# Scores of a recurrence step in two blocks of 64 queries in place of four blocks of 32

## The chip, the cores and the metric

The kernel runs on one core of one Trainium2 chip. The metric is the device time of one execution in microseconds, the median of several runs. TensorE (PE) multiplies 128x128 blocks of weights with streams of columns, and its weight loads are profiled apart as PEld. VectorE (DVE), ScalarE (ACT) and GpSimd (POOL) do the elementwise work, and SyncE (SP) issues transfers. The engines run their own programs and wait for each other on semaphores.

## What is computed

One step of a two-layer decoder trunk for 1024 prompt tokens and 64 sample tokens (8 sequences of 8). The first layer is a pooling mixer, the second gated linear attention with four heads of key width 128 and value width 512. All is float32. What the change touches is the recurrence of a head over the prompt. The reference does it in chunks of 32 tokens:

```python
bcum = jnp.cumsum(lg, axis=3)                 # log decay within a chunk
q_dec = q * jnp.exp(bcum)
k_intra = k * jnp.exp(-bcum)
k_state = k * jnp.exp(blast - bcum)
att = jnp.where(causal, jnp.einsum('nbhid,nbhjd->nbhij', q_dec, k_intra), 0.0)
o_intra = jnp.einsum('nbhij,nbhje->nbhie', att, v)
def step(s, inp):
    qc, kc, vc, dc = inp
    o_inter = jnp.einsum('bhid,bhde->bhie', qc, s)
    s = dc[..., None] * s + jnp.einsum('bhjd,bhje->bhde', kc, vc)
    return s, o_inter
```

The result does not hang on the length of the chunk: a score of query i and key j is the sum over d of q[i] k[j] exp(L[i] - L[j]), L being the running sum of the log decay. Any token's L can be taken off both sides, as long as neither exponential gets too large.

## The kernel before

Each engine has its program written out by hand, and the order in it is fixed. In the second layer a head goes through: projections of queries and keys, log decay, value rows for all tokens, then the recurrence over eight steps of 128 tokens (`SUP`), then gates, norm and output projection. The work of the heads on PE is written out four times; on the other engines the later heads are loops.

In the recurrence PE runs, for each step: a part of the gate projections as filling (`fill`), the scores of the next step (`scores(s + 1)`), a transposition of the next step's decayed keys (`key_rows`), the output of this step (`output`: scores times values, then queries times state), the state's update (`update`), another filling, and later the small products for the sample tokens. Products of the projections are split in a high and a low part of type f32r, three products each, all at L549.

The scores of a step are made in blocks of `CH` = 32 queries, so four in a step of 128. Block b has a copy of the keys of its own, `Kp[:, b, :]`, in which the decay of the keys is measured from the last token ahead of the block. Keys behind the block are zeros, set once a head by a memset of all of Kp at L960. To make a step's blocks

- ACT (`exps`, L1171) writes exp(-(L[j] - L[reference])) into the first 32 (b + 1) columns of block b, for four blocks with 32, 64, 96 and 128 columns; the first block needs no reference. It waits for PE's scores of the step before (`att_done`), since there is one Kp;
- POOL (`scale_kp`, L966) multiplies the blocks with the keys kT, four instructions of the same widths, once the last exponential is done;
- DVE (`qd_args`, L1459 and L1460) writes L[i] - L[reference] for the queries into qd, a copy for the first block and a subtraction for the other three; ACT takes the exponential (L1175), and DVE multiplies with the queries (`scale_qk`, L1468);
- PE (`scores`, L1842) multiplies each block of Kp (weights, 128x128) with its 32 columns of qd into a part of the PSUM bank X[0], four matmuls in f32, when Kp and qd are there and the scores of the step before are read;
- DVE (`att_out`, L1481) copies the causal half of the 128x128 scores to `att`.

Other work of a step on these engines: ACT evacuates gates (L1213), transposed keys (L1190) and outputs (L1202, L1203) and takes the exponential for `qs` (L1184), the queries that meet the state; DVE scales qs (L1474) and updates the state; POOL sums squares (L975, L977) and makes the low parts of weights (L344). At a head's end Kp also holds the rows of the sample tokens, all 512 columns, which are multiplied at L1924 with 64 columns of an identity. `att_hi` and `att_lo` at L1919 are the sample tokens' scores in two parts, 64 columns each. L417 is the sum of squares between the layers, matmuls with a single column.

Of the kernel before, what the change touches and what calls it, by code (L numbers as in the profile page):

```python
# [24 lines left out]
P = 128  # L25
# [13 lines left out]
WE = BUF + TP + NB * SEG  # L39
SE0 = BUF + TP  # L40
RANK = 16
CH = 32
SUP = 4 * CH
NSUP = TP // SUP
EPS = 1e-6
NC_ = 1 + NB
# [45 lines left out]
def trunk(nc, x_prompt, x_sample, c_prompt, c_sample, state_pool, state_gla, ada_w, ada_b, norm_g,  # L92
# [8 lines left out]
    with ctx:  # L101
        def sb(name, shape, dt=f32, stack=ctx):
            return stack.enter_context(nc.sbuf_tensor(name, shape, dt))
# [50 lines left out]
        S = sb("S", [P, GW])  # L154
        qd = sb("qd", [P, SUP])
        qs = sb("qs", [P, SUP])
        ks = sb("ks", [P, SUP])
        ksT = sb("ksT", [P, 2, P])
        att = sb("att", [P, 2, SUP])
        att_s = sb("att_s", [P, NS])  # L160
# [25 lines left out]
        L = sb("L", [P, T], stack=heads)  # L186
        Kp = sb("Kp", [P, 4, SUP], stack=heads)
        ki_s = sb("ki_s", [P, NS], stack=heads)
# [52 lines left out]
        def sem(name):  # L241
            return ctx.enter_context(nc.semaphore(name))
# [44 lines left out]
        kp_zero, kp_exp, kp_ready = sem("kp_zero"), sem("kp_exp"), sem("kp_ready")  # L287
# [17 lines left out]
        def units(plan, g, n):  # L305

            return g * plan.units + n + 3
# [9 lines left out]
        def wait_apart(eng, what, count):  # L317


            count = eng.to_reg(count)  # L320
            eng.wait_ge(vec_ready, 1)
            eng.wait_ge(what, count)
# [18 lines left out]
        def lo_slots(lay, plan, eng, g, j):  # L341

            eng.wait_ge(lay.hi_done, g * plan.slots + j + 1)
            nc.gpsimd.tensor_tensor(slot_lo(plan, j), stage[:, j % 2, :], slot_hi(plan, j).bitcast(f32),  # L344
                                    ALU.subtract).then_inc(lay.lo_done, 1)
# [531 lines left out]
        def _(pool):  # L877
# [71 lines left out]
            def head(g, first):  # L949
                if first:  # L950
                    pool.wait_ge(h_ready, 8)
                    pool.wait_ge(hs_low_ready, 8)
                for j in range(2 if first else 0, GP.slot["Z0"] + 1):
                    if j == GP.slot["V0"]:
                        pool.wait_ge(L1.evac[0], g * GP.in_set[0] + GP.place[GP.unit["Q"]] + 1)
                        pool.wait_ge(L1.evac[1], g * GP.in_set[1] + GP.place[GP.unit["K"]] + 1)
                    lo_slots(L1, GP, pool, g, j)

                wait_apart(pool, L1.unit_done, units(GP, g, GP.unit["LG"] + 1))
                pool.memset(Kp[:], 0.0).then_inc(kp_zero, 1)  # L960

                def scale_kp(s):

                    pool.wait_ge(kp_exp, g * NSUP + s + 1)
                    for b in range(4):
                        last = pool.tensor_tensor(Kp[:, b, 0:CH * (b + 1)], Kp[:, b, 0:CH * (b + 1)],  # L966
                                                  kT[:, s * SUP:s * SUP + CH * (b + 1)], ALU.mult)
                    last.then_inc(kp_ready, 1)

                def square_sum(s):  # L970

                    n = P if s < NSUP else NS
                    q = sqo[s % 2]
                    pool.wait_ge(osq_ready, g * (NSUP + 1) + s + 1)
                    pool.tensor_tensor(q[:, 0:2 * n], q[:, 0:2 * n], q[:, 2 * n:4 * n], ALU.add).then_inc(chain_p, 1)  # L975
                    pool.wait_ge(chain_p, s + 1)
                    pool.tensor_tensor(q[:, 0:n], q[:, 0:n], q[:, n:2 * n], ALU.add).then_inc(osum_ready, 1)  # L977

                scale_kp(0)
                lo_slots(L1, GP, pool, g, GP.slot["Z1"])  # L980
                scale_kp(1)
                for s in range(NSUP + 1):
                    if s + 2 < NSUP:
                        scale_kp(s + 2)
                    if s == 1:
                        lo_slots(L1, GP, pool, g, GP.slot["Z2"])
                    if s == 5:
                        lo_slots(L1, GP, pool, g, GP.slot["Z3"])
                    square_sum(s)
                pool.wait_ge(ksm_ready, (g + 1) * NB)  # L990
                lo_slots(L1, GP, pool, g, GP.slot["O01"])
                for j in range(GP.slot["O23"], GP.slots):
                    lo_slots(L1, GP, pool, g, j)
                pool.sem_clear(chain_p)

            head(0, True)
            with pool.Fori(1, NG) as g:
                head(g, False)
# [3 lines left out]
        def _(act):  # L1002
# [117 lines left out]
            def head(g, first):  # L1120
# [21 lines left out]
                for t, (n0, w) in enumerate(NT):  # L1142
                    last = nc.scalar.activation(L[:, n0:n0 + w], ps[GP.set[u]][:, t, 0:w], ACT.Identity,
                                                bias=vecT[:, ds(g + V_BG, 1)])
# [20 lines left out]
                def exps(s):  # L1165
                    c0 = s * SUP
                    if s >= 1:
                        act.wait_ge(att_done, g * NSUP + s)
                    for b in range(4):
                        kw = {} if b == 0 else {"bias": L[:, c0 + CH * b - 1:c0 + CH * b]}  # L1170
                        last = nc.scalar.activation(Kp[:, b, 0:CH * (b + 1)], L[:, c0:c0 + CH * (b + 1)], ACT.Exp,  # L1171
                                                    scale=-1.0, **kw)
                    last.then_inc(kp_exp, 1)
                    act.wait_ge(qd_arg, g * NSUP + s + 1)
                    nc.scalar.activation(qd[:], qd[:], ACT.Exp).then_inc(qd_exp, 1)  # L1175
                    if s >= 1:
                        act.wait_ge(kT_done, g * NSUP + s)
                    nc.scalar.activation(ks[:], L[:, c0:c0 + SUP], ACT.Exp, scale=-1.0,
                                         bias=L[:, c0 + SUP - 1:c0 + SUP]).then_inc(ks_exp, 1)
# [36 lines left out]
                def high(i):  # L1216

                    act.wait_ge(gated, g * KG + i + 1)
                    nc.scalar.activation(a_hi[:, i, :], oT[:, i, :], ACT.Copy).then_inc(gated_hi, 1)

                exps(0)
                exp_qs(0)
                split_slot(L1, GP, act, g, GP.slot["Z1"])
                act.wait_ge(smp_kT, g + 1)
                nc.scalar.activation(ksT_s[:], ps[1][:, 1, 0:P], ACT.Copy).then_inc(smp_ksT, 1)
                ksT_out(0)
                exps(1)
                for s in range(NSUP):
                    if s in (0, 4):
                        gate_in(s // 4)  # L1230
                    if s + 1 < NSUP:
                        ksT_out(s + 1)
                    if s + 2 < NSUP:
                        exps(s + 2)
                    o_out(s)
                    if s + 1 < NSUP:
                        exp_qs(s + 1)
                    if s in (1, 5):
                        split_slot(L1, GP, act, g, GP.slot["Z2"] + s // 4)
# [8 lines left out]
                                     scale=1.0 / GW)  # L1248
                nc.scalar.activation(rms_cols[0:NS, NSUP:NSUP + 1], X[0][0:NS, P + NSUP:P + NSUP + 1], ACT.Sqrt,
                                     bias=eps[0:NS, 0:1], scale=1.0 / GW).then_inc(orms_ready, 1)  # L1250
# [20 lines left out]
            for s in range(NSUP + 1):  # L1271
                n = P if s < NSUP else NS
                act.wait_ge(yT_done, s + 1)
                if s:
# [5 lines left out]
                                     scale=1.0 / D).then_inc(y_root, 1)  # L1280
# [3 lines left out]
        def _(dve):  # L1284
# [140 lines left out]
            with dve.Fori(0, NG) as g:  # L1425
# [28 lines left out]
                def qd_args(s):  # L1454

                    c0 = s * SUP
                    if s >= 1:
                        dve.wait_ge(att_done, g * NSUP + s)
                    nc.vector.tensor_copy(qd[:, 0:CH], L[:, c0:c0 + CH])  # L1459
                    nc.vector.tensor_tensor(qd[:, CH:SUP].rearrange("p (b t) -> p b t", b=3),  # L1460
                                            L[:, c0 + CH:c0 + SUP].rearrange("p (b t) -> p b t", b=3),
                                            L[:, c0 + CH - 1:c0 + SUP - 1:CH].unsqueeze(2).broadcast_to([P, 3, CH]),
                                            ALU.subtract).then_inc(qd_arg, 1)

                def scale_qk(s):
# [85 lines left out]
                att_out(0)  # L1551
                dve.wait_ge(smp_ksT, g + 1)
                qd_args(1)
                scale_qk(1)
                for s in range(NSUP + 2):
# [56 lines left out]
        def _(pe):  # L1612
# [178 lines left out]
            def head(g, first):  # L1791
# [42 lines left out]
                def scores(s):  # L1834
                    pe.wait_ge(kp_ready, g * NSUP + s + 1)
                    pe.wait_ge(qd_ready, g * NSUP + s + 1)
                    if s >= 1:
                        pe.wait_ge(att_ready, g * NSUP + s)
                    else:
                        pe.wait_ge(smp_attr, g + 1)  # L1840
                    for b in range(4):
                        last = nc.tensor.matmul(X[0][:, b * CH:(b + 1) * CH], Kp[:, b, :], qd[:, b * CH:(b + 1) * CH],  # L1842
                                                start=True, stop=True)
                    last.then_inc(att_done, 1)
# [185 lines left out]
```

## Time and profile before

| | us |
|---|---|
| median of 3 runs | 1652.73 |
| lowest and highest of the runs | 1651.33, 1653.35 |
| span of the profiled execution, first to last instruction | 1651.1 |
| PE busy in it | 1613.4 |

What lies around the span is not in the profile; the runs shown are 0.2 to 2.3 us longer than it. The layers follow each other: the pooling layer to about 750 us, norm and first projections to about 850 us, then the four heads of about 213 us each, with a recurrence of some 70 us in each, and the last norm from about 1625 us.

Matmuls are pipelined: a record lasts from the start of its matmul to the drain of its last column, so records overlap, and what one costs the engine is read from its start to the start of the next. An f32 matmul shows as two records. A wait in the trace is put down to the one that ended it last.

### The profile page before, as it was taken

Reading aid. Unit: us, or ns where it says so; the run is one execution under the profiler, and the core shown is the slowest. Engines: PE = TensorE matmul, PEld = TensorE weight load, DVE = VectorE, ACT = ScalarE, POOL = GpSimd, SP = SyncE. Lnnn points to the kernel's source line nnn. Section 1 sums busy time; section 2 is a strip of 40 time slices with the busy share of each in tenths; the row PEclk is TensorE's granted clock in tenths of the full one; section 3 lists DMA queues with packets and bytes.
Section 4 is the critical chain, followed back from the end, with each engine's and each line's share of the span. In section 5 each row is a group of like instructions: output and inputs, shape, how many; then the busy total and the mean of one; then the engine's idle time right before and its main releaser. Section 6 shows DMA issues by size and latency. Waiting matters only on the chain.

```text
span 1651.1 us, 25118 instructions
## 1 busy us (share of the span) xinstructions
PE 1613.4 (98%) x9827; PEld 1501.1 (91%) x9827; DVE 818.7 (50%) x1271; ACT 458.2 (28%) x969; POOL 375.8 (23%) x384
## 2 busy tenths in 40 slices
PE   6999999999999999998999999999999999999996
PEld 5899999999999999998788898888998989979896
DVE  4654449443944475457224562245622356224475
ACT  4321112111211121123325413154040541315423
POOL 3022212211211212211314223133130322314310
PEclk8999999999999999998999999999999999999998
DMA  9512221221122121210202212022120221201312
GB/s 330 193 56 87 62 63 42 84 74 42 55 78 64 57 67 54 77 41 27 64 18 73 84 40 77 13 64 84 53 66 12 64 96 40 77 13 40 110 37 108
DMA packets 137545, 115.03 MB, mean 70 GB/s; under 512 B 6013, under 2 KB 120281, under 8 KB 137442
## 3 DMA queue, kind: packets, MB, share of 16 engines
q1 hardware_dynamic: 135616, 112.87, 22.0%
q8 instruction: 78, 1.28, 0.3%
q10 hardware_dynamic: 1834, 0.74, 0.2%
q14 instruction: 17, 0.14, 0.0%
HBM read 99.05 MB, written 15.00 MB: 69 GB/s over the span
## 4 chain that ended last, share of the span: by engine, by line
PE 94%; DVE 3%; SPq 1%; DMA 1%; ACT 1%; issue 0%; ACTq 0%; DVEq 0%
PE psA L549 40%; PE psB L549 29%; PE psB L1804 8%; PE psA L1804 4%; PE psB L1860 2%; PE psB L1877 2%; PE psX L1842 2%; PE psB L1868 2%; PE psX L1897 1%; DVE a_hi L637 1%; PE psB L1909 1%; PE psX L1720 1%; DMA ada<-in_ada_w 1%; DVE y_rows L1606 0%; PE psB L1910 0%; PE psX L1661 0%
## 5 line engine op out<-in xcount | busy, mean ns | idle before, releaser
L344 POOL TENSOR_TENSOR w_lo<-stage,w_hi 128x1024 fp32r<-128x1024 f32 x100 | 249.7, 2496 | 891.1 <-ACT w_hi L339 891.1
L339 ACT ACTIVATE w_hi<-stage 128x1024 fp32r<-128x1024 f32 x100 | 107.0, 1070 | 433.7 <-PE psB L549 297.6
L549 PE MATMUL psA<-h_hi,w_hi 128*128 128x362 f32 (+1 forms) x864 | 210.9, 349 | 4.1 <-DVE h_lo L453 3.8
L549 PE MATMUL psA<-h_lo,w_hi 128*128 128x362 f32 (+1 forms) x864 | 193.6, 329 | 0.0
L549 PE MATMUL psA<-h_hi,w_lo 128*128 128x362 f32 (+1 forms) x864 | 193.1, 329 | 0.0
L549 PEld LDWEIGHTS psA<-h_hi,w_hi 128*128 128x128 f32 x864 | 151.4, 190 | 27.1 <-issue 21.2
L549 PEld LDWEIGHTS psA<-h_hi,w_lo 128*128 128x128 f32 x864 | 151.5, 190 | 0.0
L549 PEld LDWEIGHTS psA<-h_lo,w_hi 128*128 128x128 f32 x864 | 151.4, 190 | 0.0
L549 PE MATMUL psA<-a_hi,w_hi 128*128 128x362 f32 (+1 forms) x480 | 109.7, 334 | 2.6 <-DVE a_lo L640 1.9
L549 PE MATMUL psB<-h_hi,w_hi 128*128 128x362 f32 (+1 forms) x480 | 109.7, 331 | 0.0
L549 PE MATMUL psB<-h_hi,w_lo 128*128 128x362 f32 (+1 forms) x480 | 107.9, 327 | 0.0
L549 PE MATMUL psB<-h_lo,w_hi 128*128 128x362 f32 (+1 forms) x480 | 107.7, 327 | 0.0
L549 PE MATMUL psA<-a_hi,w_lo 128*128 128x362 f32 (+1 forms) x480 | 106.4, 327 | 0.0
L549 PE MATMUL psA<-a_lo,w_hi 128*128 128x362 f32 (+1 forms) x480 | 106.4, 327 | 0.0
L549 PE MATMUL psB<-a_hi,w_hi 128*128 128x362 f32 (+1 forms) x480 | 106.0, 329 | 0.0
L549 PE MATMUL psB<-a_hi,w_lo 128*128 128x362 f32 (+1 forms) x480 | 105.2, 327 | 0.0
L549 PE MATMUL psB<-a_lo,w_hi 128*128 128x362 f32 (+1 forms) x480 | 105.1, 327 | 0.0
L966 POOL TENSOR_TENSOR Kp<-Kp,kT 128x32 f32<-128x32 f32 (+3 forms) x128 | 45.5, 385 | 219.2 <-ACT Kp L1171 219.2
L549 PEld LDWEIGHTS psA<-a_hi,w_hi 128*128 128x128 f32 x480 | 82.7, 188 | 7.3 <-DVE a_lo L640 4.7
L549 PEld LDWEIGHTS psB<-h_hi,w_hi 128*128 128x128 f32 x480 | 82.9, 189 | 2.5 <-issue 2.4
L549 PEld LDWEIGHTS psB<-h_hi,w_lo 128*128 128x128 f32 x480 | 83.7, 188 | 0.0
L549 PEld LDWEIGHTS psB<-h_lo,w_hi 128*128 128x128 f32 x480 | 83.5, 188 | 0.0
(345 smaller groups left out, 2790.6 us busy)
## 6 DMA issues: line engine op xcount, KB each, us to landing
stage<-in_gla_w_in SPq DMA_DIRECT2D x40, 512.0 KB, 3.8
stage<-in_pool_w_in SPq DMA_DIRECT2D x32, 512.0 KB, 4.1
ada_stage<-in_ada_w SPq DMA_DIRECT2D x24, 512.0 KB, 3.8
ada<-in_ada_w SPq DMA_DIRECT2D x16, 512.0 KB, 8.4
stage<-in_pool_w_out SPq DMA_DIRECT2D x16, 512.0 KB, 3.4
v<-in_state_gla SPq DMA_DIRECT2D x32, 256.0 KB, 2.6
out_new_gla_sample<-v SPq DMA_DIRECT2D x32, 256.0 KB, 2.1
stage<-in_gla_w_out SPq DMA_DIRECT2D x16, 512.0 KB, 3.7
```

Of the source, the lines that this page charges most:

```text
L339: nc.scalar.activation(slot_hi(plan, j), stage[:, j % 2, :], ACT.Copy).then_inc(lay.hi_done, 1)
L344: nc.gpsimd.tensor_tensor(slot_lo(plan, j), stage[:, j % 2, :], slot_hi(plan, j).bitcast(f32), ALU.subtract).then_inc(lay.lo_done, 1)
L549: last = nc.tensor.matmul(ps[u][:, t, 0:width], weight(w[:, p, :], k), a[:, k, n0:n0 + width], start=(k == 0 and pas == 0), stop=(k == kt ...
L637: nc.vector.tensor_copy(a_hi[:, i, c], oT[:, i, c]).then_inc(chain_v, 1)
L966: last = pool.tensor_tensor(Kp[:, b, 0:CH * (b + 1)], Kp[:, b, 0:CH * (b + 1)], kT[:, s * SUP:s * SUP + CH * (b + 1)], ALU.mult)
L1720: last = nc.tensor.matmul(X[1][rows, P:2 * P], csT[:, k * NC_:k * NC_ + CG], ada_stage[:, k, :], start=(k < 4), stop=(k >= 4))
L1804: last = nc.tensor.matmul(ps[GP.set[u]][0:n, j, :], h[:, k, s * P:s * P + n], w[k // 2][:, c], start=(k == 0 and pas == 0), stop=(k == KD ...
L1842: last = nc.tensor.matmul(X[0][:, b * CH:(b + 1) * CH], Kp[:, b, :], qd[:, b * CH:(b + 1) * CH], start=True, stop=True)
L1860: last = nc.tensor.matmul(ps[1][:, 0, e * P:(e + 1) * P], v[:, s, e * P:(e + 1) * P], att[:, s % 2, :], start=(e == 0), stop=(s == 0 and e ...
L1868: last = nc.tensor.matmul(ps[1][:, 0, e * P:(e + 1) * P], S[:, e * P:(e + 1) * P], qs[:], start=False, stop=(e == KG - 1), skip_group_chec ...
L1877: nc.tensor.matmul(ps[1][:, 2, :], ksT[:, s % 2, :], v[:, s, :], start=True, stop=True).then_inc(upd_done, 1)
L1897: last = nc.tensor.matmul(X[1][rows, :], qd_cols[:, c:c + CG], v[:, b, :], start=first, stop=not first)
```

## The change

A block has 64 queries in place of 32, so a step of 128 tokens has two blocks. The decay of both keys and queries of a block is measured from the middle token of the block (`MID` = 31), in place of the token ahead of it, so that no exponent spans more than 32 tokens, as before. Blocks 2 and 3 of Kp are no longer written in a step; the tile keeps its size, since the sample tokens' rows need it. The memset covers only what is never written: columns 64 to 127 of block 0.

```diff
-CH = 32
-SUP = 4 * CH
+CH = 64
+MID = CH // 2 - 1
+SUP = 2 * CH
...
-                pool.memset(Kp[:], 0.0).then_inc(kp_zero, 1)
+                pool.memset(Kp[:, 0, CH:SUP], 0.0).then_inc(kp_zero, 1)
...
-                    for b in range(4):
+                    for b in range(2):
                         last = pool.tensor_tensor(Kp[:, b, 0:CH * (b + 1)], Kp[:, b, 0:CH * (b + 1)],
                                                   kT[:, s * SUP:s * SUP + CH * (b + 1)], ALU.mult)
...
-                    for b in range(4):
-                        kw = {} if b == 0 else {"bias": L[:, c0 + CH * b - 1:c0 + CH * b]}
+                    for b in range(2):
+                        mid = c0 + CH * b + MID
                         last = nc.scalar.activation(Kp[:, b, 0:CH * (b + 1)], L[:, c0:c0 + CH * (b + 1)], ACT.Exp,
-                                                    scale=-1.0, **kw)
+                                                    scale=-1.0, bias=L[:, mid:mid + 1])
...
-                    nc.vector.tensor_copy(qd[:, 0:CH], L[:, c0:c0 + CH])
-                    nc.vector.tensor_tensor(qd[:, CH:SUP].rearrange("p (b t) -> p b t", b=3),
-                                            L[:, c0 + CH:c0 + SUP].rearrange("p (b t) -> p b t", b=3),
-                                            L[:, c0 + CH - 1:c0 + SUP - 1:CH].unsqueeze(2).broadcast_to([P, 3, CH]),
+                    nc.vector.tensor_tensor(qd[:].rearrange("p (b t) -> p b t", b=2),
+                                            L[:, c0:c0 + SUP].rearrange("p (b t) -> p b t", b=2),
+                                            L[:, c0 + MID:c0 + SUP:CH].unsqueeze(2).broadcast_to([P, 2, CH]),
                                             ALU.subtract).then_inc(qd_arg, 1)
...
-                    for b in range(4):
+                    for b in range(2):
                         last = nc.tensor.matmul(X[0][:, b * CH:(b + 1) * CH], Kp[:, b, :], qd[:, b * CH:(b + 1) * CH],
                                                 start=True, stop=True)
```

PE's program around the scores of a step in the middle of a recurrence, before; psX is the bank of the scores, the line after them transposes the decayed keys:

```order
L549 MATMUL psA<-h_hi,w_lo 128x362 x2
L1842 MATMUL psX<-qd,Kp 128x32 x4
L1852 MATMUL psB<-ident,ks 128x128
L1860 MATMUL psB<-att,v 128x128 x4
L1868 MATMUL psB<-qs,S 128x128 x4
L1877 MATMUL psB<-v,ksT 128x512
```

The same place now:

```order
L550 MATMUL psA<-h_hi,w_lo 128x362 x2
L1842 MATMUL psX<-qd,Kp 128x64 x2
L1852 MATMUL psB<-ident,ks 128x128
L1860 MATMUL psB<-att,v 128x128 x4
L1868 MATMUL psB<-qs,S 128x128 x4
L1877 MATMUL psB<-v,ksT 128x512
```

Four matmuls of 32 columns have become two of 64; nothing before or behind them has moved.

POOL's program where it makes the blocks of steps 0 and 1, before:

```order
L960 MEMSET Kp 128x512
L966 TENSOR_TENSOR Kp<-Kp,kT 128x32
L966 TENSOR_TENSOR Kp<-Kp,kT 128x64
L966 TENSOR_TENSOR Kp<-Kp,kT 128x96
L966 TENSOR_TENSOR Kp<-Kp,kT 128x128
L344 TENSOR_TENSOR w_lo<-stage,w_hi 128x1024
```

and now:

```order
L961 MEMSET Kp 128x64
L967 TENSOR_TENSOR Kp<-Kp,kT 128x64
L967 TENSOR_TENSOR Kp<-Kp,kT 128x128
L345 TENSOR_TENSOR w_lo<-stage,w_hi 128x1024
L967 TENSOR_TENSOR Kp<-Kp,kT 128x64
```

The blocks of 32 and 96 columns are gone on POOL, and likewise on ACT; the order of the rest stays.

## Rows read from the trace of the kernel before

**Rows 1.** The page, busy time of each engine (share of the span), instructions:

```profile
PE 1613.4 (98%) x9827; PEld 1501.1 (91%) x9827; DVE 818.7 (50%) x1271; ACT 458.2 (28%) x969; POOL 375.8 (23%) x384
```

**Rows 2.** Windows of the recurrences: stretch, length, busy by engine, PEclk, DMA share, GB/s:

```profile
850.00:925.00 75.00, 75.00 (x492) 66.67 (x491) 31.69 (x86) 36.43 (x95) 26.73 (x48) 1.00 0.24 78
...
1489.00:1564.00 75.00, 75.00 (x492) 66.67 (x491) 31.49 (x86) 36.54 (x95) 26.69 (x49) 1.00 0.24 78
```

**Rows 3.** Waits of PE from 800 to 1640 us: total us, times, longest:

```profile
PE psB L1804 <- ACT kT L1127: 1.4, 3, 0.5
```

**Rows 4.** Groups of PE by shape, 850 to 1640 us: busy us, mean ns, idle before:

```profile
L1842 PE MATMUL psX<-qd,Kp 128*128 128x32 f32 x256 | 31.1, 265 | 0.0
```

**Rows 5.** Timeline of PE in the last head's recurrence: start us, length us, instruction:

```profile
1500.79 0.97 PE L1842 MATMUL psX<-qd,Kp 128*128 128x32 f32 x8
...
1506.47 0.97 PE L1842 MATMUL psX<-qd,Kp 128*128 128x32 f32 x8
1507.28 0.31 PE L1852 MATMUL psB<-ident,ks 128*128 128x128 f32 x1
...
1508.31 1.06 PE L1868 MATMUL psB<-qs,S 128*128 128x128 f32 x8
...
1513.27 0.97 PE L1842 MATMUL psX<-qd,Kp 128*128 128x32 f32 x8
```

**Rows 6.** Timeline of PE at the third recurrence's end, matmuls of 64 columns:

```profile
1348.01 0.19 PE L1919 MATMUL psX<-att_hi,v_s 128*128 128x64 f32 x1
1348.04 0.27 PE L1919 MATMUL psX<-att_lo,v_s 128*128 128x64 f32 x1
...
1348.82 1.08 PE L1924 MATMUL psX<-ident,Kp 128*128 128x64 f32 x8
1349.71 0.47 PE L1909 MATMUL psB<-v_s,ksm 128*128 128x512 f32 x1
```

**Rows 7.** Groups by shape in the last head, 1430 to 1640 us, as in rows 4:

```profile
L1171 ACT ACTIVATE Kp<-L 128x128 f32<-128x128 f32 x8 | 3.1, 388 | 0.0
L1171 ACT ACTIVATE Kp<-L 128x64 f32<-128x64 f32 x8 | 2.7, 336 | 0.0
L1468 DVE TENSOR_TENSOR qd<-qd,qT 128x128 f32<-128x128 f32 x8 | 2.3, 290 | 9.6 <-ACT qd L1175 9.6
L1460 DVE TENSOR_TENSOR qd<-L 128x96 f32<-128x96 f32 x8 | 2.0, 251 | 0.0
L1459 DVE COPY qd<-L 128x32 f32<-128x32 f32 x8 | 1.5, 182 | 0.0
...
L966 POOL TENSOR_TENSOR Kp<-Kp,kT 128x128 f32<-128x128 f32 x8 | 3.6, 455 | 0.0
L966 POOL TENSOR_TENSOR Kp<-Kp,kT 128x64 f32<-128x64 f32 x8 | 3.2, 404 | 0.0
```

**Rows 8.** Timeline of ACT ahead of step 2 of the last head:

```profile
1500.98 1.20 ACT L1213 ACTIVATE PQ<-psA 128x364 f32<-128x364 f32 x3 [1.49 <-PE psA L549]
...
1503.67 1.03 ACT L1171 ACTIVATE Kp<-L 128x32 f32<-128x32 f32 x4
1504.60 0.29 ACT L1175 ACTIVATE qd<-qd 128x128 f32<-128x128 f32 x1
```

**Rows 9.** Timeline of POOL, products for steps 2 and 3 of the last head:

```profile
1504.78 1.45 POOL L966 TENSOR_TENSOR Kp<-Kp,kT 128x32 f32<-128x32 f32 x4 [5.55 <-ACT Kp L1171]
...
1508.88 1.44 POOL L966 TENSOR_TENSOR Kp<-Kp,kT 128x32 f32<-128x32 f32 x4 [1.44 <-ACT Kp L1171]
```

**Rows 10.** Timeline of DVE, queries of step 1 for the state:

```profile
1506.38 0.68 DVE L1474 TENSOR_TENSOR qs<-qs,qT 128x128 f32<-128x128 f32 x1 [0.23 <-ACT qs L1184]
```

**Rows 11.** Between the layers: timeline of PE (one row), then windows as in rows 2:

```profile
748.50 5.18 PE L417 MATMUL psX<-ones,PQ 128*128 128x1 f32 x36
...
750.00:755.00 5.00, 3.68 (x24) 3.55 (x24) 0.76 (x4) 0.47 (x3) 2.35 (x1) 0.65 0.00 0
...
765.00:770.00 5.00, 5.00 (x23) 5.00 (x22) 4.97 (x6) 2.30 (x2) 0.00 (x0) 0.65 0.00 0
```

## What the change will do to the time

> **What bounds the kernel now.** I read the page's busy times first, then the windows of the recurrence, then who waits for whom on PE, then single rows of the timelines. PE is busy for 98% of the span and no other engine for more than half of it, beside the weight loads that belong to PE [rows 1]. What an average hides is told by the windows: there are four recurrences, one per head, and in the first and in the last of them (the other two read the same) PE is busy 75.00 of 75.00 us at a granted clock of 1.00 [rows 2]. From 800 to 1640 us PE has one entry under waits that is not in the program's last transposes, 1.4 us in three times, and it stands in the value projections, not in the recurrence [rows 3]. So in a step PE waits for nobody. Whatever time a step gives back must come out of PE's own queue, and it comes back whole only as long as nobody else becomes late.
>
> **What the scores cost PE.** A step has four f32 matmuls of 32 columns, and each shows as two records, so 256 records in 4 heads x 8 steps [rows 4]. Their mean of 265 ns is no price: records overlap, since each includes the drain of its matmul. The price is start to start. The eight records of one step start at 1506.47 and the transposition behind them starts at 1507.28 [rows 5]: 0.81 us a step, about 26 us in the run.
>
> Is that 0.81 us made of columns or of weight loads? Each of the four matmuls loads its own 128x128 block of Kp. Had it been columns, 128 columns would cost the same in two pieces as in four. The nearest row has exactly the new form: f32 matmuls of 128x64 at the end of the recurrence, eight records from 1348.82 to 1349.71, 0.89 us or 0.111 us a record [rows 6]. The eight 32-column records take 0.81 us, nearly as long with half the columns. So a record's price hangs on its weight load, not on its columns, up to 64 of them at least. The missing 0.08 us is the first record. Behind a matmul of another kind its weights are already there: in the 64-column row ahead of those, the first record starts at 1348.01 and the second at 1348.04, 0.03 us, while the next seven take (1348.82 - 1348.04) / 7 = 0.111 us [rows 6]. With 0.03 + 7 x 0.111 the scores of a step come to 0.81 us, as seen.
>
> The new step has two matmuls, four records: first + 3 x 0.111 us. The first record is bounded by 0.03 us (as it is now) and 0.11 us (as if its load were not hidden). I take 0.06 us: a record whose weights wait for it has only its columns to move, and those double. That makes 0.39 us a step in place of 0.81, a gain of 0.42 us, with ends of 0.36 and 0.45. Times 32 steps: **13.4 us, between 11.5 and 14.4**.
>
> A rule speaks against this. The Trainium skill's page "TensorE: Matmul & The Clock Gate", section "Step-by-step: what each phase is for", has it that one column enters per cycle and that throughput is therefore purely N cycles. By it four times 32 and two times 64 columns cost the same and the sum would be zero; the rows above speak against it for a stream in which every matmul brings new weights.
>
> **What the change does elsewhere.** *ACT* runs two exponentials a step for Kp in place of four. The four start at 1503.67 and what follows them at 1504.60, 0.93 us [rows 8]. The two that stay have the forms that exist today, 336 and 388 ns by their own durations [rows 7], which overlap as PE's do; so they take between half of 0.93 (0.47) and 0.72 us, and Kp's exponentials end 0.21 to 0.46 us earlier. The bias column of the first block is new there; of the blocks with a bias today the 64-wide one is the 336 ns. *POOL* multiplies two blocks with k in place of four: 1.45 us today [rows 9] against 404 + 455 = 859 ns [rows 7], 0.59 us less. Its clearing of Kp once a head shrinks from 512 columns to 64; POOL is busy 23% of the span [rows 1] and PE does not come to step 0 until value projections and gates have run, so I cost it at nothing. *DVE* loses a copy (182 ns) and widens its subtraction from 96 columns (251 ns) to 128; the nearest row of that width is 290 ns [rows 7], so the pair gets about 0.14 us shorter. DVE then idles for ACT's exponential of qd, 9.6 us in the eight steps of a head [rows 7], so this is hidden whichever way it falls. Nothing moves in any queue, no DMA is touched, Kp keeps its place and size.
>
> None of this is on PE's path, but it is the cover that has to hold. The tightest place is step 2 of every head. POOL's last product for it ends at 1504.78 + 1.45 = 1506.23 [rows 9] and PE reaches these scores at 1506.47 [rows 5]: 0.24 us of room. The chain to it begins with the gate's evacuation on ACT at 1500.98 [rows 8], which waits for the Z0 product ahead of the scores of step 1, at 1500.79 [rows 5]. Between there and step 2 PE does one step's scores, so PE will arrive 0.42 us earlier. ACT and POOL arrive 0.21 + 0.59 = 0.80 us earlier at least. Room after: 0.24 - 0.42 + 0.80 = 0.6 us or more. Next tightest is the output of step 1: qs is ready at 1506.38 + 0.68 = 1507.06 [rows 10], and PE wants it at 1508.31 [rows 5], 1.25 us later. Two steps' scores lie ahead of it since 1500.79, so 0.84 us of the room goes and 0.41 us stay even if ACT gained nothing. In step 3 POOL is done at 1508.88 + 1.44 = 1510.32 [rows 9] and PE comes at 1513.27 [rows 5], 2.9 us. No PE wait appears.
>
> **Rivals.**
> - *Columns are what is paid.* Then the scores keep their 0.81 us a step, and the time stays where it is, 1652.7 us. The pace of 0.111 us in rows of 64 columns against 0.10 in those of 32 speaks against it. The change would then halve the matmuls and not their cost. The rule of the Trainium skill's page "TensorE: Matmul & The Clock Gate" (section "Step-by-step: what each phase is for"), taken as it stands, says just this.
> - *The ring takes part of it back.* If ACT and POOL gained nothing at all, PE would wait 0.42 - 0.24 = 0.18 us at step 2 of each head, 0.7 us in all. If steps 1 and 2 of each head gave back all that they gain, 8 x 0.42 = 3.4 us go and 10.0 remain: 1642.7 us. For it: the 0.24 us of room. Against: the same edit shortens just the two engines that this wait hangs on.
> - *Slower: PE's clock falls in the recurrence.* The trace has a stretch in which it fell: after matmuls of a single column (36 of them take 5.18 us from 748.50) and waits between the layers, the granted clock read 0.65 from 750 and still 0.65 to 770 us, part of it at the lower level of 1.2 GHz [rows 11]. If a wait at step 2 opened and dropped the clock so in each head, 4 x 20 us x 0.35 = 28 us would be lost: 1652.7 - 13.4 + 28 = 1667 us. It decides from 13.4 + 3.3 us lost, 12 us of such a clock a head. Against it: the recurrence runs at 1.00 throughout, with scores of 32 columns; now they move 64 columns in the same 0.11 us, and no wait of PE's is in sight.
>
> **How the numbers follow.** The profiled execution spans 1651.1 us; the three runs shown lie 0.2 to 2.3 us above that, with a median of 1652.73. The sum against the span is 1651.1 - 13.4 = 1637.7, and what lies around it stays, so against the median it is 1652.73 - 13.4 = **1639.3 us**.
>
> Chances: the forecast 0.86; the ring taking a part 0.08 (still faster); columns 0.03 (no change); the clock 0.02, and 0.01 for something slower that I do not see. A measurement of this kernel can tell about 0.2%, 3.3 us, from no change. So faster 0.94, same 0.03, slower 0.03. For the range: from the fastest run shown less the largest gain, 1651.3 - 14.4 = 1636.9, to the slowest less the smallest gain, 1653.4 - 11.5 = 1641.9; that holds the forecast. I stretch it to **1636.5 to 1643.0**, so that the ring's 1642.7 lies in it too.
>
> **What would show it right or wrong.** In the changed profile the scores' line has 128 records of 128x64, and from the first of a step to the transposition behind it lie 0.36 to 0.45 us. 0.8 us there means columns. PE reads 98% busy again, the recurrence of a head is 8 x 0.42 = 3.4 us shorter, and from 800 to 1640 us PE's waits do not grow. The stretches ahead of 850 us keep their times. If a wait of PE's for Kp or qs appears, in step 1 or 2 first, the ring rival is at work, and if the granted clock in the recurrence is under 1.00, the last one. The forecast would be wrong by its size if the first record of a step costs otherwise than 0.06 us, and by its sign only if the clock goes.

## The result: 1639.0 us, as forecast

The changed kernel takes 1638.99 us in the median of four runs (1636.88 to 1641.13), the kernel before 1652.06 us beside it (1651.33 to 1653.35). The ratio is 0.9916, with a 95% interval of 0.9901 to 0.993. The forecast was 1639.3 us.

The profiled execution is the longest of the four runs, 1641.13 us with a span of 1638.7. Its page, busy time of each engine (answers to [rows 1]):

```profile
PE 1601.3 (98%) x9699; PEld 1487.4 (91%) x9699; DVE 819.3 (50%) x1239; ACT 446.9 (27%) x905; POOL 356.3 (22%) x320
```

PE lost 128 records and 12.1 us of busy time, and is as full as before. Windows of the four recurrences, columns as in [rows 2]:

```profile
850.00:925.00 75.00, 75.00 (x481) 66.66 (x480) 35.75 (x82) 35.94 (x82) 24.52 (x36) 1.00 0.26 82
...
1489.00:1564.00 75.00, 75.00 (x473) 66.58 (x472) 38.42 (x75) 38.59 (x83) 22.35 (x33) 1.00 0.24 81
```

PE is busy throughout and its granted clock stays at 1.00. (The last window now reaches a little past the recurrence.) Timeline of PE at step 2 of the last head, the place of [rows 5]:

```profile
1496.33 0.65 PE L550 MATMUL psA<-h_hi,w_lo 128*128 128x364 f32 x3
1496.82 0.55 PE L1842 MATMUL psX<-qd,Kp 128*128 128x64 f32 x4
1497.21 0.28 PE L1852 MATMUL psB<-ident,ks 128*128 128x128 f32 x1
1497.33 1.06 PE L1860 MATMUL psB<-att,v 128*128 128x128 f32 x8
```

From the first score record to the transposition lie 1497.21 - 1496.82 = 0.39 us, where there were 0.81. The scores' line in both kernels, with the starts of its first and its last record, before and then after:

```profile
L1842 PE MATMUL psX<-qd,Kp x256: 190/276/276, 856.5 to 1545.2; 128*128 128x32 f32 x128
```

```profile
L1842 PE MATMUL psX<-qd,Kp x128: 217/275/275, 858.1 to 1532.9; 128*128 128x64 f32 x128
```

Between the first and the last scores lie 1545.2 - 856.5 = 688.7 us before and 1532.9 - 858.1 = 674.8 us after, 13.9 us less. What a step gains is read inside a recurrence. Timeline of PE, scores of steps 0 and 7 of the last head, before and then after:

```profile
1495.37 0.97 PE L1842 MATMUL psX<-qd,Kp 128*128 128x32 f32 x8
...
1544.52 0.97 PE L1842 MATMUL psX<-qd,Kp 128*128 128x32 f32 x8
```

```profile
1486.61 0.55 PE L1842 MATMUL psX<-qd,Kp 128*128 128x64 f32 x4
...
1532.64 0.55 PE L1842 MATMUL psX<-qd,Kp 128*128 128x64 f32 x4
```

49.15 us have become 46.03, 3.12 us less over seven steps and the same in each of the four heads: 0.446 us a step, 14.3 us in 32. The first scores come 1.6 us later. PE does the same work ahead of them in both kernels, and the first 60 us of this execution ran at a granted clock of 0.89 against 0.91, which by its size is most of it. So this one pair of spans shows 12.4 us where the medians show 13.1.

### The profile page after: what moved, and what is told of

Same layout as the page of the kernel before. It is cut to its first block, busy times and chain, and to the rows that moved or that the text cites. A ratio compares the mean times of both kernels' runs of the same rounds, so it can differ in the third digit from the quotient of the medians.

```text
span 1638.7 us, 24702 instructions
## 1 busy us (share of the span) xinstructions
PE 1601.3 (98%) x9699; PEld 1487.4 (91%) x9699; DVE 819.3 (50%) x1239; ACT 446.9 (27%) x905; POOL 356.3 (22%) x320
## 4 chain that ended last, share of the span: by engine, by line
PE 94%; DVE 3%; SPq 1%; DMA 1%; ACT 1%; issue 0%; ACTq 0%; DVEq 0%
PE psA L550 40%; PE psB L550 29%; PE psB L1804 8%; PE psA L1804 4%; PE psB L1860 2%; PE psB L1877 2%; PE psB L1868 2%; PE psX L1897 1%; DVE a_hi L638 1%; PE psX L1842 1%; PE psB L1909 1%; PE psX L1720 1%; DMA ada<-in_ada_w 1%; DVE y_rows L1606 0%; PE psB L1910 0%; PE psX L1661 0%
## 5 line engine op out<-in xcount | busy, mean ns | idle before, releaser
L550 PEld LDWEIGHTS psB<-a_hi,w_hi 128*128 128x128 f32 x480 | 82.7, 188 | 0.9 <-issue 0.8
```

Source lines behind the costliest of these rows:

```text
L550: last = nc.tensor.matmul(ps[u][:, t, 0:width], weight(w[:, p, :], k), a[:, k, n0:n0 + width], start=(k == 0 and pas == 0), stop=(k == kt ...
```

## The experiments

The later runs shared a chip with fresh runs of the kernel before, whose median lay between 1653.8 and 1655.7 us. So each is compared by its ratio to before, and sizes under 1 us are read from the traces. The changed kernel was run once more as their measure.

> The changed kernel once more, as the measure for the three beside it. Every theory: 1639 us, within 2 us; 0.39 us from the first score record of a step to the transposition; no PE wait between 850 and 1620 us.

Measured: 1639.21 us, 0.9913 of before (0.9899 to 0.9926), 0.39 us for the scores, and no wait of PE's in the recurrences.

### Four loads again, all else as changed

```diff
-                    for b in range(2):
-                        last = nc.tensor.matmul(X[0][:, b * CH:(b + 1) * CH], Kp[:, b, :], qd[:, b * CH:(b + 1) * CH],
+                    for b in range(4):
+                        last = nc.tensor.matmul(X[0][:, b * 32:(b + 1) * 32], Kp[:, b // 2, :], qd[:, b * 32:(b + 1) * 32],
```

> The changed kernel, with ACT, POOL and DVE as changed, but PE makes the scores of a step in four matmuls of 32 columns again, each block of Kp loaded twice. Theory 'weight loads' (the price of the scores is the number of weight loads): 0.81 us a step again, all of the gain gone, 1652 to 1653 us. Theory 'columns' (128 columns cost the same in any number of matmuls): 0.39 us, 1639 us. Theory 'elementwise' (the gain came from the shorter chain on ACT, POOL and DVE): 1639 us, whatever PE's rows show.

Measured: 1653.57 us, 0.9998 of before (0.9988 to 1.0007). The gain is gone, although ACT, POOL and DVE do the changed kernel's work. Timeline of PE at step 0 of the last head:

```profile
1495.52 0.97 PE L1842 MATMUL psX<-qd,Kp 128*128 128x32 f32 x8
1496.33 0.31 PE L1852 MATMUL psB<-ident,ks 128*128 128x128 f32 x1
```

0.81 us again, for the same 128 columns and the same weights, only loaded twice each. Of the three theories just the one of weight loads stands: columns cannot be the price, and the shorter chain on the other engines gave nothing by itself: steps 0 to 7 of the last head take as long as before, 49.2 us. The run does not tell a load's price from a price that any matmul has, whatever it loads, since each matmul brings one load; that is taken up below.

### The old work back on ACT and POOL

```diff
+                    for b, w in ((2, 32), (3, 96)):
+                        nc.scalar.activation(Kp[:, b, 0:w], L[:, c0:c0 + w], ACT.Exp, scale=-1.0,
+                                             bias=L[:, c0 + MID:c0 + MID + 1])
...
+                    for b, w in ((2, 32), (3, 96)):
+                        pool.tensor_tensor(Kp[:, b, 0:w], Kp[:, b, 0:w], kT[:, s * SUP:s * SUP + w], ALU.mult)
```

> The changed kernel with PE as changed, but ACT and POOL get back, ahead of their two blocks, two instructions each of 32 and 96 columns, written into blocks of Kp that nobody reads. 'Weight loads': the gain stays. From the changed kernel's trace POOL is done 0.85 us ahead of PE at step 2; the extra work takes 0.38 us on ACT and 0.66 us on POOL, so PE waits about 0.2 us at step 2 of each head and nowhere else: 0.8 us in all, 1639.8 us. 'Elementwise': the gain goes, 1652 us.

Measured: 1639.77 us, 0.9924 (0.991 to 0.9938), which overlaps the changed kernel's. The trace is sharper. Waits of PE in the recurrences (total, times, longest), then its timeline at step 2 of the first head, with the weight loads (PEld) of the scores:

```profile
PE psX L1847 <- POOL Kp L969: 0.7, 4, 0.2
```

```profile
866.71 0.65 PE L550 MATMUL psA<-h_hi,w_lo 128*128 128x364 f32 x3
867.55 0.66 PE L1847 MATMUL psX<-qd,Kp 128*128 128x64 f32 x4 [0.18 <-POOL Kp L969]
868.04 0.28 PE L1857 MATMUL psB<-ident,ks 128*128 128x128 f32 x1
```

```profile
867.54 0.52 PEld L1847 LDWEIGHTS psX<-qd,Kp 128*128 128x128 f32 x4 [0.48 <-POOL Kp L969]
```

The wait is where it was expected, once a head, and the profile gives it 0.18 us, the figure that the prediction had for a ring that gains nothing. PE loses more than that. The scores start 867.55 - 866.71 = 0.84 us after the three records ahead of them, in place of 0.49, and take 868.04 - 867.55 = 0.49 us in place of 0.39. The first load starts with the scores themselves, at 867.54; without a wait it starts 0.16 us ahead of them, behind the matmul before (1496.66 against 1496.82 in the changed kernel). That is 0.35 + 0.10 = 0.45 us a head, 1.8 us in four, and the ratios differ by as much (0.9924 against 0.9913), though their intervals overlap. So without the edits on ACT and POOL step 2 would have been late, and those edits closed it. They are worth 1.8 us and not the gain.

### Twice the extra work

The same with four extra instructions on each engine.

```diff
+                    for b, i, w in ((2, 0, 32), (3, 0, 96), (3, 96, 32), (2, 32, 96)):
+                        nc.scalar.activation(Kp[:, b, i:i + w], L[:, c0:c0 + w], ACT.Exp, scale=-1.0,
+                                             bias=L[:, c0 + MID:c0 + MID + 1])
...
+                    for b, i, w in ((2, 0, 32), (3, 0, 96), (3, 96, 32), (2, 32, 96)):
+                        pool.tensor_tensor(Kp[:, b, i:i + w], Kp[:, b, i:i + w], kT[:, s * SUP:s * SUP + w], ALU.mult)
```

> The changed kernel with twice the extra work of the run with two instructions: ACT and POOL get four unread instructions each, of 32, 96, 32 and 96 columns, ahead of their two. With two the products came 0.85 + 0.18 = 1.03 us later against PE at step 2. 'Weight loads' with the ring as the cover: 2.06 us later now, less the 0.85 us of room, so a wait of 1.2 us at step 2 of each head, none above 0.3 us in other steps, 4.8 us in all, 1644 us, and the clock stays at 1.00 in the recurrence. Rival 'clock': a wait of this size lets the granted clock fall behind it, and the run loses 10 us or more, 1650 us.

Measured: 1648.09 us, 0.9959 (0.9945 to 0.9973). Waits of PE, the first recurrence's window, then PE's timeline at step 2 of the first head:

```profile
PE psX L1847 <- POOL Kp L969: 4.8, 4, 1.2
...
PE psB L1914 <- DVE S L1498: 1.3, 4, 0.3
```

```profile
850.00:925.00 75.00, 73.48 (x470) 64.81 (x470) 34.69 (x80) 40.94 (x109) 32.62 (x64) 1.00 0.25 81
```

```profile
866.18 0.65 PE L550 MATMUL psA<-h_hi,w_lo 128*128 128x364 f32 x3
868.03 0.66 PE L1847 MATMUL psX<-qd,Kp 128*128 128x64 f32 x4 [1.20 <-POOL Kp L969]
868.53 0.28 PE L1857 MATMUL psB<-ident,ks 128*128 128x128 f32 x1
```

The 4.8 us of waits stand as expected. A second wait, 0.3 us a head in the sample tokens' update behind the state, was not foreseen. The clock stayed at 1.00 across waits of 1.2 us, so the clock rival finds nothing here up to that size; a longer wait wasn't tried. The time lost is again more than the waits: at step 2 it is 868.03 - 866.18 - 0.49 = 1.36 us to the start of the scores and 0.11 us in them, 1.47 us a head, and the second wait costs some 0.36. Steps 0 to 7 of a head take 47.86 us in place of 46.03. Four times 1.83 us are 7.3 us, and 0.9913 of 1655.3 and 7.3 us are 1648.2 us, against 1648.1 measured. The 4.8 us that were expected to be lost were 2.5 us short: they counted the wait and not what it does to the loads behind it, and had no second wait.

### One block of 128

```diff
-CH = 64
+CH = 128
-SUP = 2 * CH
+SUP = CH
...
-                pool.memset(Kp[:, 0, CH:SUP], 0.0).then_inc(kp_zero, 1)
+                pool.sem_inc(kp_zero, 1)
...
-                    for b in range(2):
+                    for b in range(1):
...
-                    nc.vector.tensor_tensor(qd[:].rearrange("p (b t) -> p b t", b=2),
-                                            L[:, c0:c0 + SUP].rearrange("p (b t) -> p b t", b=2),
-                                            L[:, c0 + MID:c0 + SUP:CH].unsqueeze(2).broadcast_to([P, 2, CH]),
+                    nc.vector.tensor_tensor(qd[:], L[:, c0:c0 + SUP],
+                                            L[:, c0 + MID:c0 + MID + 1].broadcast_to([P, SUP]),
                                             ALU.subtract).then_inc(qd_arg, 1)
```

The loop of one block stands on ACT, POOL and PE.

> One block of 128 queries: one matmul a step, decay from the middle of 128 tokens, one exponential on ACT, one product on POOL, no clearing of Kp. 'Weight loads': two records, of which the first streams 128 columns behind weights that are already there (0.11 us) and the second pays its load (0.11 us): 0.22 us a step in place of 0.39, 32 x 0.17 = 5.4 us less than the changed kernel, 1633.6 us. 'Columns': 1639 us. 'Elementwise': a gain of the size that ACT and POOL lose, less than 0.6 us a head, so 1637 us at best.

Measured: 1634.85 us, 0.988 (0.9864 to 0.9895), clear of the changed kernel. Timeline of PE at step 1 of the last head:

```profile
1489.33 0.38 PE L1841 MATMUL psX<-qd,Kp 128*128 128x128 f32 x2
1489.55 0.27 PE L1851 MATMUL psB<-ident,ks 128*128 128x128 f32 x1
1489.66 1.06 PE L1859 MATMUL psB<-att,v 128*128 128x128 f32 x8
```

0.22 us, as the sum of a first record that only streams its columns (0.11) and a second that pays its load (0.11) had it. This is faster than both kernels. Its exponents span up to 64 tokens of decay in place of 32, which a model with stronger decay would have to afford.

### Fewer weights per load

If loads are the price, smaller loads should be cheaper. Half of block 0's keys lie behind all of its queries, and their scores are never read.

```diff
-                        last = nc.tensor.matmul(X[0][:, b * CH:(b + 1) * CH], Kp[:, b, :], qd[:, b * CH:(b + 1) * CH],
+                        last = nc.tensor.matmul(X[0][0:CH * (b + 1), b * CH:(b + 1) * CH], Kp[:, b, 0:CH * (b + 1)], qd[:, b * CH:(b + 1) * CH],
```

The same line was put into the changed kernel (loads of 64 and 128 columns) and into the kernel before (32, 64, 96 and 128).

> The changed kernel, but the first block of a step loads only its own 64 keys as weights (the other 64 are behind all of its queries, and the causal copy never reads their scores). Theory 'load by columns' (a record's price is the columns of its weight load): the second record falls from 0.111 to about 0.056 us, and the first is still hidden; 0.39 becomes 0.33 us a step, 1.8 us less, 1637.3 us. Rival 'one price per matmul' (0.111 us for any f32 record, however few weights): 0.39 us, 1639.2 us.

> The kernel before, with its four blocks of 32 queries, but block b loads only its first 32 (b + 1) keys as weights; the scores left out are behind the queries and never read. 'Load by columns': 2 x (32 + 64 + 96 + 128) columns at 0.111 us per 128 are 0.56 us, the first record a little less: 0.53 to 0.56 us in place of 0.81, 8 to 9 us less than before, 1644 to 1646 us. 'One price per matmul': 0.81 us and 1653.8 us.

Measured: 1645.01 us, 0.9942 (0.9925 to 0.9959), and 1656.34 us, 1.0013 (1.0003 to 1.0024). Both are slower than what they were cut from, which no theory had. Timeline of PE in the trimmed changed kernel at step 1 of the last head, then in the trimmed old one:

```profile
1495.58 0.66 PE L550 MATMUL psA<-h_hi,w_lo 128*128 128x364 f32 x3
1496.16 0.69 PE L1842 MATMUL psX<-qd,Kp 128*64 128x64 f32 x4
1496.69 0.28 PE L1852 MATMUL psB<-ident,ks 128*128 128x128 f32 x1
```

```profile
1502.76 0.66 PE L549 MATMUL psA<-h_hi,w_lo 128*128 128x364 f32 x3
1503.34 0.99 PE L1842 MATMUL psX<-qd,Kp 128*32 128x32 f32 x8
1504.16 0.30 PE L1852 MATMUL psB<-ident,ks 128*128 128x128 f32 x1
```

The scores take 0.53 us in the first, where full loads take 0.39, and 0.82 in the second, where full loads take 0.81. And the three records ahead of them now last 0.58 us to the scores' start in both; in the changed kernel it is 1496.82 - 1496.33 = 0.49. The weight loads of the trimmed changed kernel (PEld, busy us, mean ns, idle before) say where the 0.09 us are:

```profile
L1842 PEld LDWEIGHTS psX<-qd,Kp 128*128 128x128 f32 x64 | 9.5, 188 | 2.2
L1842 PEld LDWEIGHTS psX<-qd,Kp 128*64 128x64 f32 x64 | 6.1, 135 | 7.3 <-issue 7.3
```

The load of 64 columns is shorter itself, 135 against 188 ns, but the weight loader idles 7.3 us in front of 32 steps, 0.23 us each, with no wait that the profile shows.

The old kernel's records, one by one, settle what the run with four loads left open. The second record of a matmul starts 0.053 us after its first where 32 columns are loaded, 0.079 for 64, 0.106 for 96 and 0.112 for 128, with 32 columns streamed each time. So the price does rise with the load, and 'one price per matmul' is out. What the shorter loads gain is lost again at each change: the first record with 64, 96 and 128 loaded columns starts 0.126, 0.152 and 0.085 us after the one ahead of it.

The theory that came of it: a load of another width than the one before it is not hidden behind the running matmul. To tell this from a load that is never hidden when it is short, all loads of the scores were made 64 wide:

```diff
-                    for b in range(2):
-                        last = nc.tensor.matmul(X[0][:, b * CH:(b + 1) * CH], Kp[:, b, :], qd[:, b * CH:(b + 1) * CH],
+                    for b, k in ((0, 0), (1, 0), (1, 1)):
+                        last = nc.tensor.matmul(X[0][k * CH:(k + 1) * CH, b * CH:(b + 1) * CH],
+                                                Kp[:, b, k * CH:(k + 1) * CH], qd[:, b * CH:(b + 1) * CH],
```

> The changed kernel, with the scores of a step in three matmuls that load 64 keys each (the first half for both blocks, the second half for the second block), where the run before mixed loads of 64 and 128. Theory 'change of width' (loads are priced by their columns, and a load of another width than the one before it starts only when the matmul ahead has streamed): one such start at the beginning of a step and one at the transposition; six records of 0.055 us between them; the last record of the matmul ahead lasts 0.25 us to the next start in place of 0.16, and 0.42 us lie from the first score record to the transposition. Per step 0.12 us more than the changed kernel, 4 us in the run: about 1643 us, 0.994 of before. Rival 'a short load is never hidden' (each load under 128 columns waits for the matmul ahead): 0.11 us a record or more, 0.64 us, 10 us more than the changed kernel, 1649 us, 0.998 of before.

Measured: 1645.41 us, 0.9946 (0.9929 to 0.9962). Timeline of PE at step 1 of the last head:

```profile
1493.23 0.65 PE L550 MATMUL psA<-h_hi,w_lo 128*128 128x364 f32 x3
1493.81 0.45 PE L1842 MATMUL psX<-qd,Kp 128*64 128x64 f32 x6
1494.18 0.33 PE L1853 MATMUL psB<-ident,ks 128*128 128x128 f32 x1
1494.35 1.06 PE L1861 MATMUL psB<-att,v 128*128 128x128 f32 x8
```

Six records in 0.37 us, 0.06 each in the mean, so the rival's 0.64 us did not come. The mean is no price of a short load, though: record by record the starts lie 0.013, 0.093, 0.014, 0.045, 0.058 and 0.153 us apart, and the record that raises the scores' semaphore, which the last matmul carries, is the fourth to start. So records of the two halves seem to run side by side.

Time is lost around the short loads: 0.58 in place of 0.49 us ahead of the scores, and 0.17 in place of 0.12 us from the transposition to the output. Together that is 0.58 + 0.37 + 0.17 = 1.12 us against 0.49 + 0.39 + 0.12 = 1.00, the 0.12 us a step that were expected. The sum is made up otherwise, though: the scores were to take 0.42 us, and the 0.05 behind the transposition were in no term.

That the change of width as such is what costs is not shown, and two places of the changed kernel's trace speak against it. Timeline of PE ahead of the low-rank product between the projections (L1786), where the weights go from 128 columns to 32, then ahead of the last head's log decay (L1814), whose weights have all 128 columns but only 32 rows:

```profile
790.04 0.33 PE L550 MATMUL psB<-h_lo,w_hi 128*128 128x362 f32 x1
790.21 0.33 PE L550 MATMUL psB<-h_hi,w_lo 128*128 128x362 f32 x1
790.38 0.33 PE L1786 MATMUL psX<-h_hi,w_gl_hl 128*32 128x364 f32 x1
```

```profile
1426.70 0.65 PE L550 MATMUL psB<-h_hi,w_lo 128*128 128x364 f32 x3
1427.28 0.88 PE L1814 MATMUL psA<-PQ,w_up 32*128 32x364 f32 x6
```

The change of width in the first costs nothing: the starts lie 0.17 us apart, as those ahead of it do. In the second the start is late by the same 0.09 us (0.58 in place of 0.49) with no change of width. The weights in the first (`w_gl_hl`) are of type f32r, those in the second (`w_up`) and those of the scores f32. So the late loads here are f32 loads that fill a part of the array, or stand right behind one. What holds them back stays open.

## Why the prediction was right, step by step

- **The bound.** "Whatever time a step gives back must come out of PE's own queue" holds: with PE's four loads back, nothing is left of the gain; with the other engines' work back, all but 1.8 us of it is still there.
- **What is paid.** The price per weight load and not per column was read from 64-column rows elsewhere in the trace [rows 6]. The same 128 columns took 0.81 us in four matmuls, 0.39 in two and 0.22 in one, and the trimmed loads show that it is the load that costs, at 0.053 to 0.112 us by its columns. The Trainium skill's page "TensorE: Matmul & The Clock Gate" (section "Step-by-step: what each phase is for") has throughput as purely N cycles. By it the three would be equal, which they are not where every matmul brings new weights. Where the load is hidden, in the first record of a step, the time does go with the columns: 0.028 us for 32, 0.055 for 64 and 0.108 for 128, some two cycles of 2.4 GHz a column in f32.
- **The first record.** Taken at 0.06 us between ends of 0.03 and 0.11; the step came out at 0.39 us and its first record at 0.055, so the value taken was right. Its source was not: the 0.03 us was read from a row of 64 columns [rows 6], which by the prediction's own argument should have been the new form's value as it stood. That row's matmuls (`att_hi`, `att_lo`, type f32r) show one record each, and its 64 columns take what 32 take in f32. That the two agreed was luck, worth 1 us in the sum.
- **A term that was missing.** The transposition behind the scores got cheaper: 1507.42 - 1507.28 = 0.14 us before [rows 5] for the first of these, and 1497.33 - 1497.21 = 0.12 us after, 0.027 us less before rounding. Before, the row behind it reads:

```profile
1507.42 1.06 PE L1860 MATMUL psB<-att,v 128*128 128x128 f32 x8
```

  In 32 steps that is some 0.9 us that the sum did not have; with it, 14.3 us, as the recurrences show (0.446 us a step; 8 steps of a head 3.6 us shorter, where 3.4 were forecast). The medians show 13.1, and runs of one kernel differ by some 4 us, so the median cannot tell 13.4 from 14.3. That it came within 0.3 us of the forecast is luck; the price of the scores, 0.42 us a step, is not.
- **ACT, POOL and DVE.** Two exponentials take 1495.01 - 1494.46 = 0.55 us (bounds 0.47 and 0.72) and two products 0.79 us (0.86 from the durations). The wider subtraction on DVE came to 345 ns in the mean where the row of its width had 290, still 88 ns less than the pair that it replaces, and hidden. Timeline of ACT, timeline of POOL and DVE's group:

```profile
1494.46 0.64 ACT L1172 ACTIVATE Kp<-L 128x64 f32<-128x64 f32 x2
1495.01 0.30 ACT L1176 ACTIVATE qd<-qd 128x128 f32<-128x128 f32 x1
```

```profile
1495.18 0.79 POOL L967 TENSOR_TENSOR Kp<-Kp,kT 128x64 f32<-128x64 f32 x2 [6.20 <-ACT Kp L1172]
```

```profile
L1460 DVE TENSOR_TENSOR qd<-L 128x128 f32<-128x128 f32 x8 | 2.8, 345 | 0.0
```

- **The cover.** "0.6 us or more" of room at step 2: POOL is done at 1495.18 + 0.79 = 1495.97 and PE comes at 1496.82, 0.85 us. But Kp is the weights, so what POOL must be ahead of is their load. Timeline of PEld at step 2 of the last head, before and then after:

```profile
1506.30 1.02 PEld L1842 LDWEIGHTS psX<-qd,Kp 128*128 128x128 f32 x8
```

```profile
1496.66 0.58 PEld L1842 LDWEIGHTS psX<-qd,Kp 128*128 128x128 f32 x4
```

  The room was 1506.30 - 1506.23 = 0.07 us before, where the prediction had 0.24, and is 0.69 us now. No wait came, since ACT and POOL gained more than PE did.
- **The rivals.** Columns are out by the run with four loads. The ring exists and is worth 1.8 us, within its bound of 3.4 us. The prediction priced it at 0.7 us, because it took the room at the matmul and not at its load (0.42 - 0.07 = 0.35 us late, not 0.18) and left out that the first load is then no longer hidden (0.10 us). The clock never left 1.00 in a recurrence, not with waits of 1.2 us either.

## What to carry to other kernels

On an engine that never waits, price a matmul by the start-to-start time of rows that have its form and its neighbours; the mean length of a record (265 ns here, for 101) says nothing. Where each small matmul brings new weights, merging queries under one set of weights pays even though no column is saved, here up to 128 columns. Then go down the list of those who feed the merged matmul: the tenths that they gain or lose decide whether PE keeps the rest. Take their room at the load, if they make the weights: a wait of 0.18 us in the profile cost 0.45 us here.

## What the runs showed that was not expected

- Loads of fewer weight columns made the kernel slower, though each load is shorter: in f32, the first short load behind the split products started the scores about 0.09 us late, with the loader idle for 0.23 us and no wait that the profile shows. In f32r a change of width cost nothing. Cutting unread keys from Kp's blocks cost 0.29% of the run (0.9942 against 0.9913) in the changed kernel.
- A wait for weights costs more than the idle time in the profile: 0.45 us for 0.18, and 1.47 us for 1.20.
- The time from the transposition to the output's first matmul differs with the scores ahead of it: 0.14 us behind matmuls of 32 columns, 0.12 behind 64, 0.11 behind 128.
